# Expert choice in two batches, TensorE products that nothing reads, and a later read of the latent weights

## What is computed

```
h = h + pool_mixer(rmsnorm(h, a_norm)) ; h = h + hierarchical_moe(rmsnorm(h, ffn_norm[0]), ...)
k_nope, k_rope, v = shared_latent_kv(h, ...)
h = h + mla_mixer(rmsnorm(h, b_norm), ...) ; h = h + hierarchical_moe(rmsnorm(h, ffn_norm[1]), ...)
return rmsnorm(h, final_norm)[:, 16:]

# hierarchical_moe, the part that chooses
p_g = softmax(xf @ wr_g + br_g); g_sel = argmax(p_g); w_g = max(p_g)
sel = logit_e[g_sel]                      # 8 of the 32 experts' logits
top_v, top_i = top_k(sel, 2)
gate = w_g * softmax(top_v); eid = g_sel * 8 + top_i
# then rows are sorted by expert, every expert runs on its rows, and each token adds its two results
```

## Time and profile before

| what | value |
|---|---|
| median of 3 runs | 2169.54 us |
| the profiled execution's own time | 2170.03 us |
| its span, first to last instruction | 2168.3 us |
| PE busy | 1961.4 us (90%) |
| DVE busy | 809.5 us (37%) |
| ACT busy | 531.4 us (25%) |
| mean granted TensorE clock | 0.944 |

### The profile page before, as it was taken

One profiled execution on the slowest core, in us unless ns is written; L12 is line 12 of the kernel. 1 busy time (PEld: TensorE's weight loads), 2 busy tenths in 40 slices (PEclk: granted clock), 3 DMA queues, 4 the chain that ended last, 5 costly groups with the idle time before them and its releaser, 6 DMA issues. The chain is left out here.

```text
span 2168.3 us, 28117 instructions
## 1 busy us (share of the span) xinstructions
PE 1961.4 (90%) x10975; PEld 1146.7 (53%) x10975; DVE 809.5 (37%) x1863; ACT 531.4 (25%) x1290; POOL 189.3 (9%) x283
## 2 busy tenths in 40 slices
PE   8999999889997958999976999999999985999990
PEld 4545554478543944444434656777675553444440
DVE  1114556766353452111115534434352124111115
ACT  1003233433111311111122433333331110111112
POOL 0000002001162201000002000000000000000003
PEclk9999999889998967999998999999999986999995
DMA  3500100020021146999984000000010026999987
GB/s 136 213 34 11 39 20 4 1 81 4 2 98 44 49 204 245 404 423 425 424 368 158 23 1 1 1 1 1 1 78 23 29 81 278 379 426 423 425 354 263
DMA packets 51388, 334.66 MB, mean 154 GB/s; under 512 B 6832, under 2 KB 7152, under 8 KB 33200
## 3 DMA queue, kind: packets, MB, share of 16 engines
q1 hardware_dynamic: 39376, 289.63, 32.9%
q0 software_dynamic: 11872, 43.13, 5.5%
HBM read 285.48 MB, written 47.25 MB: 153 GB/s over the span
## 5 line engine op out<-in xcount | busy, mean ns | idle before, releaser
L221 PE MATMUL psum<-arena 128*128 128x512 f32 (+12 forms) x9584 | 1817.1, 384 | 117.5 <-DVE arena L2052 26.7
L221 PEld LDWEIGHTS psum<-arena 128*128 128x128 f32 (+3 forms) x9584 | 994.5, 169 | 887.3 <-issue 774.8
L2162 DVE TENSOR_TENSOR arena<-psum,arena 128x256 f32<-128x256 f32 x50 | 21.2, 425 | 429.5 <-ACT arena L2212 429.5
L1541 ACT ACTIVATE arena<-arena 128x1024 f32<-128x1024 f32 x43 | 45.4, 1056 | 255.1 <-DVE arena L2907 105.6
L2248 POOL DMA_INDIRECT arena<-xn_rows,arena x50 | 47.3, 945 | 672.4 <-PE psum L2123 447.9
L2212 ACT ACTIVATE arena<-psum 128x256 f32<-128x256 f32 x50 | 19.3, 385 | 327.6 <-PE psum L221 327.6
L2820 ACT ACTIVATE arena<-psum,arena 128x1024 f32<-128x1024 f32 (+8 forms) x72 | 50.2, 699 | 188.6 <-DVE arena L2856 188.6
L1242 ACT ACTIVATE arena<-psum 128x256 f32<-128x256 f32 (+3 forms) x128 | 44.0, 356 | 103.3 <-PE psum L221 92.2
L2205 ACT ACTIVATE arena<-psum 128x512 f32<-128x512 f32 x50 | 29.9, 597 | 148.0 <-PE psum L221 148.0
L2123 PE MATMUL psum<-arena 128*128 128x128 f32 x400 | 53.7, 279 | 10.0 <-DMA arena<-xn_rows,arena 10.0
L2849 DVE TENSOR_TENSOR psum<-psum,arena 128x128 f32<-128x128 f32 (+2 forms) x72 | 20.3, 283 | 103.5 <-PE psum L221 103.2
(11 more groups left out here) (304 smaller groups left out, 1303.4 us busy)
## 6 DMA issues: line engine op xcount, KB each, us to landing
arena<-in_w_exp SPq DMA_DIRECT2D x64, 2048.0 KB, 20.0
arena<-in_w_exp SPq DMA_DIRECT2D x64, 1024.0 KB, 19.9
expert_rows<-arena SPq DMA_DIRECT2D x66, 512.0 KB, 15.3
arena<-in_x SPq DMA_DIRECT2D x16, 512.0 KB, 4.1
xn_rows<-arena SPq DMA_DIRECT2D x16, 512.0 KB, 2.6
arena<-in_w_out SPq DMA_DIRECT2D x8, 512.0 KB, 7.7
arena<-in_w_o SPq DMA_DIRECT2D x1, 4096.0 KB, 13.1
out<-arena SPq DMA_DIRECT2D x8, 512.0 KB, 5.6
```

The lines of the kernel that those rows point to most:

```text
L221: return e.matmul(out, lhsT, rhs, start=start, stop=stop, skip_group_check=True)
L1541: return e.activation(junk, h[:, s, :], ACT.Square, accum_out=sq_sum[:, s:s + 1])
```

## The change

1. `dve_table`'s first half becomes `dve_select(e, y, a, b)`, which works on the tiles a to b. It is called twice: for 0 to `first` (6 in layer 0, 7 in layer 1) inside the routing loop, and for the rest after it. The gates become `dve_gates`, after the second call, with one reciprocal in place of two. ScalarE does four exponentials in place of two.
2. TensorE gets `keep_busy`: n products of the identity with itself, four times side by side (512 columns), into bank 7, which nothing reads. Five stand ahead of the rank products, once all banks of the routing loop are empty; eleven behind the counts; five behind the index products; in layer 0 thirteen more after the last expert block.
3. `sp_latent_behind` moves behind SP's wait for the expert count and waits for the gathered rows of the first two tiles. DVE scales these weights ahead of the combines of tiles 4 and 5 in place of 2 and 3.

```diff
+            y.first = 6 if layer == 0 else 7
...
+        def dve_select(e, y, a, b):
+            ns = b - a
+            at = slice(a, b)
...
+            e.memset(y.gp[:, at, :], NEG).then_inc(*V.up())
+            after()
+            e.wait_ge(*y.rb.empty(("lg", y.slots.index(b - 1))))
...
+            if a == 0:
+                e.memset(y.before[:, 0, :], 0.0).then_inc(*V.up())
+            for s in range(a, b):
+                after()
+                e.tensor_tensor(y.before[:, s + 1, :], y.before[:, s, :], y.both[:, s, :], ALU.add).then_inc(
+                    *(y.before_in if s == y.ns - 1 else V).up())
+
+        def dve_gates(e, y):
...
+            e.wait_ge(*y.exp.at(4))
+            e.tensor_reduce(y.wg, y.eg, AX.X, ALU.add).then_inc(*V.up())
+            e.tensor_scalar(y.rr, y.e1, 1.0, None, ALU.add).then_inc(*V.up())
...
+            dve_select(e, y, y.first, ns)
+            dve_gates(e, y)
...
         def act_table(e, y):
-            for t, n in ((y.eg, 1), (y.e1, 2)):
-                e.wait_ge(*y.to_exp.at(n))
-                e.activation(t, t, ACT.Exp).then_inc(*y.exp.up())
+            for n, at in enumerate((slice(0, y.first), slice(y.first, y.ns))):
+                for u, t in enumerate((y.eg[:, at, :], y.e1[:, at])):
+                    e.wait_ge(*y.to_exp.at(2 * n + u + 1))
+                    e.activation(t, t, ACT.Exp).then_inc(*y.exp.up())
+
+        def keep_busy(e, bank, n):
+
+            for _ in range(n):
+                mm(e, four(bank), ident, bc_mid(ident, 4), True, True)
 
         def pe_table(e, y):
             ns = y.ns
+            wait_all(e, y.rb.totals)
+            keep_busy(e, banks[7], 5)
             e.wait_ge(*y.ids_g.at(2))
             e.wait_ge(*y.before_in.at(1))
...
             mm(e, y.tb.bank["count"][:, 0:NE], ones, y.before[:, ns, :], True, True).then_inc(*y.tb.fill("count"))
+            keep_busy(e, banks[7], 11)
             for s in range(ns):
...
             m.then_inc(*y.tb.fill("idx"))
+            keep_busy(e, banks[7], 5)
...
         def sp_latent_behind(e):
...
+            for s in range(2):
+                for j in range(2):
+                    e.wait_ge(*m_cl[s][j])
             e.dma_start(w_uq, io["w_uq"]).then_inc(d_lu.sem, 16)
...
             sp_store(e, y, NM - 1)
-            if y.n == 0:
-                sp_latent_behind(e)
...
-                if (d, s) == (0, 2):
+                if (d, s) == (0, 4):
                     e.wait_ge(*m_lu)
...
-                if (d, s) == (0, 3):
+                if (d, s) == (0, 5):
                     e.wait_ge(*m_uk)
...
             pe_experts(e, y)
+            if y.n == 0:
+                wait_all(e, y.ex.totals)
+                keep_busy(e, banks[7], 13)
             pe_over(e, y)
...
                 dve_route(e, y, d, p)
+                if (d, p) == ((y.norm_at, y.ns - 1) if y.n == 0 else (y.norm_at + 2, y.ns - 2)):
+                    dve_select(e, y, 0, y.first)
             dve_table(e, y)
...
             sp_over(e, y)
+            if y.n == 0:
+                sp_latent_behind(e)
```

More of the change, by code:

```diff
@@ L1686, in plan_layer @@
             else:
-                y.to_exp, y.exp, y.hot = layers[0].to_exp.after(2), layers[0].exp.after(2), layers[0].hot.after(2 * NS)
+                y.to_exp, y.exp, y.hot = layers[0].to_exp.after(4), layers[0].exp.after(4), layers[0].hot.after(2 * NS)
                 y.before_in, y.m_cnt, y.sorted = layers[0].before_in.after(1), layers[0].m_cnt.after(1), layers[0].sorted.after(NE // 8)
@@ new lines, in dve_gates, with after @@
+        def dve_gates(e, y):
+            ns = y.ns
+            def after():
+                e.wait_ge(*V.last())
+            e.wait_ge(*y.exp.at(4))
+            e.tensor_reduce(y.wg, y.eg, AX.X, ALU.add).then_inc(*V.up())
+            e.tensor_scalar(y.rr, y.e1, 1.0, None, ALU.add).then_inc(*V.up())
+            after()
+            e.tensor_tensor(y.rr, y.rr, y.wg, ALU.mult).then_inc(*V.up())
+            after()
+            e.reciprocal(y.rr, y.rr).then_inc(*V.up())
+            after()
+            e.tensor_copy(gates[:, 0:ns, 0:1], y.rr.unsqueeze(2)).then_inc(*V.up())
+            e.tensor_tensor(gates[:, 0:ns, 1:2], y.rr.unsqueeze(2), y.e1.unsqueeze(2), ALU.mult).then_inc(*V.up())
@@ L1923, in after @@
                 e.wait_ge(*V.last())
-            def largest(x):
-                for s in range(ns):
-                    e.max(y.m8[:, s, :], x[:, s, :]).then_inc(*V.up())
-                for s in range(ns):
-                    if s == 0:
-                        after()
-                    e.max_index(y.i8[:, s, :].bitcast(U32), y.m8[:, s, :], x[:, s, :]).then_inc(*V.up())
-            e.memset(y.gp, NEG).then_inc(*V.up())
-            after()
-            e.wait_ge(*y.rb.empty(("lg", y.ns - 1)))
@@ L1954, in dve_table @@
-            largest(y.me)
-            after()
-            v0, v1 = (y.m8[:, :, j:j + 1].rearrange("p a b -> p (a b)") for j in range(2))
-            e.tensor_tensor(y.e1, v1, v0, ALU.subtract).then_inc(*y.to_exp.up())
-            e.wait_ge(*y.exp.at(2))
-            e.tensor_scalar(y.rr, y.e1, 1.0, None, ALU.add).then_inc(*V.up())
-            after()
-            e.reciprocal(y.rr, y.rr).then_inc(*V.up())
-            after()
-            e.tensor_tensor(y.rr, y.rr, y.wg, ALU.mult).then_inc(*V.up())
@@ L1964, in dve_table @@
-            after()
-            e.tensor_copy(gates[:, 0:ns, 0:1], y.rr.unsqueeze(2)).then_inc(*V.up())
-            e.tensor_tensor(gates[:, 0:ns, 1:2], y.rr.unsqueeze(2), y.e1.unsqueeze(2), ALU.mult).then_inc(*V.up())
-            e.tensor_copy(y.ei, y.i8[:, :, 0:2].bitcast(U32)).then_inc(*V.up())
-            for j in range(2):
-                after()
-                e.tensor_tensor(y.oh[j], bc_mid(y.io32, ns), y.ei[:, :, j:j + 1].to_broadcast([P, ns, NE]), ALU.is_equal).then_inc(*V.up())
-                after()
-                e.tensor_tensor(y.oh[j], y.oh[j], bc_last(y.valid, NE), ALU.mult).then_inc(*V.up())
@@ L1973, in dve_table @@
-            after()
-            e.tensor_tensor(y.both, y.oh[0], y.oh[1], ALU.add).then_inc(*V.up())
-            e.memset(y.before[:, 0, :], 0.0).then_inc(*V.up())
-            for s in range(ns):
-                after()
-                e.tensor_tensor(y.before[:, s + 1, :], y.before[:, s, :], y.both[:, s, :], ALU.add).then_inc(
-                    *(y.before_in if s == ns - 1 else V).up())
+            dve_select(e, y, y.first, ns)
+            dve_gates(e, y)
             def eight(r, left):
```

53 lines of the change are left out of this document (35 added, 18 removed).

## The result

The changed kernel took 2147.68 us (median of 4 runs, 2144.10 to 2152.09), the kernel before 2169.90 in the same comparison. The ratio is 0.9903, 95% interval 0.988 to 0.9926: faster, by about 1%. The profiled execution took 2145.41 us, its span is 2143.7 against 2168.3. So the two profiled executions differ by 24.6 us, the medians by 22.2; the forecast was 17.1. PE is now busy for 2004.4 us (94%), DVE for 812.5, and the mean granted clock is 0.964 instead of 0.944.

What follows compares the result with a forecast made beforehand. PE's waits for DVE's chain in both tables and at the latent start bound the kernel; in expert blocks PE and DMA nearly tie. 7.8 + 5.9 + 3.4 = 17.1 us gave 2152.4 us, range 2145.5 to 2160.

Steps and rivals of the forecast that it cites:

- three signs that the forecast itself named for being wrong: PEclk 0.5 through the eleven products; first gathers of 8 us or more; first block's lead still there at blocks' end.
- Choice in two batches, layer 0: Layer 0's table: six tiles chosen early, three after; running counts ready at 792.4 instead of 799.2 us.
- The five ahead of the ranks: Before the rank products: raise the clock, ranks take 1.2 instead of 2.45 us; layer 0's DVE goes on 6.8 us earlier.
- Eleven: Behind the counts: need 9.7 us within a 13.85 us gap, hidden; nothing would be longer without them.
- The last five: Behind layer 0's index products: delay PE 1.5 us, warm start saves 4.0; only 1.0 us of lead counted, bounds 0 and 2.5.
- rival (a): PE, not the reads, sets the end of the expert blocks, so the remaining lead passes: 2149.9 us; chance 0.15.
- Latent weights: Latent start: first gathers faster without weight reads beside them, tile 0's combine ends 5.9 us earlier; bounds 0 and 7.
- Thirteen: After layer 0's last expert block: clock expected to have fallen again before the latent transposes; value 0, at best 3 us.
- rival (b): The thirteen products do keep the clock up into the latent stage: 3 us more, 2149.4 us; chance 0.05.
- Layer 1: Layer 1's table and first blocks: rank copy 2.9 us earlier plus 0.5 from the last five, 3.4 us.
- Rival (d): Identity products do not raise the clock in the tables, so the kernel gets slower: 2183.5 us; chance 0.03.

Runs made afterwards that it cites:

- e4: Changed kernel without the five products ahead of the ranks, in both layers: 2145.26 us, ratio 0.9868 to the kernel before.
- e8: Changed kernel with six tiles chosen first in layer 1 and only the last five products kept: 2151.73 us, ratio 0.9906 to the kernel before.
- e1: Changed kernel with all added identity products removed in both layers: 2157.53 us, ratio 0.9928 to the kernel before.
- e2: Changed kernel without the five products behind the index products, in both layers: 2156.78 us, ratio 0.9924 to the kernel before.
- e3: Changed kernel with ten products instead of five behind the index products, in both layers: 2159.42 us, ratio 0.9939 to the kernel before.
- e6: Changed kernel with latent weights again read behind the last expert store and scaled ahead of tiles 2 and 3: 2155.81 us, ratio 0.9927 to the kernel before.
- e7: Changed kernel whose latent weight reads do not wait for the first two tiles' gathered rows: 2155.36 us, ratio 0.9926 to the kernel before.
- e10: e9 without the thirteen products: 2146.16 us, ratio 0.9884 to the kernel before.
- e9: Changed kernel without the five products ahead of the ranks and with six tiles chosen first in layer 1: 2146.58 us, ratio 0.9889 to the kernel before.
- e5: The changed kernel itself, unaltered, run again: 2149.17 us, ratio 0.9903 to the kernel before.
- e11: e9 with twelve products for eleven and a small identity product behind each index product but the last: 2153.60 us, ratio 0.9911 to the kernel before.
- e12: e9 with four products instead of five behind the index products: 2144.72 us, ratio 0.9879 to the kernel before.

## Why the prediction was right, and where it was off

**Direction, path and order of size** were right: 17.1 us forecast, 22.2 measured. But one of the three signs that the forecast itself named for being wrong came true: the first block's lead is still there at the end of the blocks. Term by term:

- *Choice in two batches, layer 0.* Rank copy 6.8 us earlier, forecast 6.8. The counts were ready at 9.8 + 5.6 = 15.4 us after the last normalized row's start (forecast 15.7), the five products began at 785.44 and the copy came 2.8 us behind the counts.
- *The five ahead of the ranks.* Counted as free in layer 0 and as 3 us of the price in layer 1. e4 shows what they are: a loss of 0.3 and 1.6 us. The forecast had the numbers for this (794.85 without them against 794.8 with) and did not draw the conclusion.
- *Eleven.* Hidden, as forecast, but not quite worthless: "if they were not there nothing would be longer" is off by 0.7 to 0.8 us of A (e8); e1 against e2, with the first five's 0.3 us allowed for, gives 0.5. In layer 1 it holds.
- *The last five, and the step that failed*: "The reads' own train starts with the gathered rows, 6.8 us early. It already hands over at the last moment, so of this lead I count 1.0 us". All of it passed: A fell by 10.5 us, B did not grow. Only the fourth expert's read waits for gathered rows; the next is issued when PE is done with a buffer. It went out at 842.22 before and at 830.58 after, 11.64 us earlier, just as the second block's transposes; the fourth expert's own, at 832.67 before and 823.64 after, came only 9.03 us earlier and held nothing back. Every read behind it is tied to PE in the same way, so a read that lands 0.1 us before its block does so after any shift. The price of the delay was 0.6 us against 1.5 forecast, and the gain of the warm start 4.0, as forecast; the term is 10.5 - 6.8 = 3.7 instead of 1.0. Of the 2.7 us between them 1.5 are the lead counted as given back, 0.9 the smaller delay and 0.3 the cast, which was 7.1 us early and not 6.8. This was rival (a), with 0.15; e2 and e3 decide for it. Its own wording, that the 0.6 us wait at 1087 would go, was wrong: it is still there.
- *Latent weights.* 7.3 instead of 5.9, just outside the bounds (0 to 7). The gathers gave what was forecast: 4.3 us for the first and 1.4 for the second, forecast 4.2 and 1.7. The missing 1.6 us come with the last store, which landed that much sooner, a step that the forecast did not have. Seven of the eleven profiles without reads beside the gathers have the early landing; in the other four C is 16.4 to 17.2, that is 5.0 to 5.9 us won. e6 and e7 show the cause as forecast.
- *Thirteen.* 0 was forecast, and e10 against e9 agrees (D 28.0 and 28.3, medians 0.4 us apart). The forecast's reason does not hold throughout: it expected 4.9 us between their end and the transposes and a clock fallen by then (before the change it had fallen 4.0 us after PE's last product, not under 4); the wait was 3.4 us, and in three profiles, both of the changed kernel among them, the clock had not fallen (1.09 us), in five it had (1.97). Since D is 28.2 to 28.3 in those three and 30.5 to 30.9 in those five, a worth of up to 2.3 us in some executions is not excluded, which is rival (b). The Trainium skill, "TensorE: Matmul & The Clock Gate", section "HAM oscillation", says that a burst behind a long wait starts cold each time; over waits of 3.2 to 3.5 us the traces agree with it in three profiles of six, and over the waits of 5.6 and 5.7 us (e2, e4) in both.
- *Layer 1.* 4.9 us to the second transposes, and 0.8 in the blocks, where a wait of 1.6 us for a read shrank to 0.7: 5.7 against 3.4. The 0.8 are chance (F is 286.3 to 289.7 over all runs). The rank copy was 3.3 us early (2.9 forecast); the rest is again the lead that passed.
- *Rival (d)* is out: the clock rose in each group of identity products. The Trainium skill, "TensorE: Matmul & The Clock Gate", section "PE-mode transpose", says that transpose mode does not count as busy for the clock; that concerns another mode, and no run here tests it.

Sum by measured terms: 10.5 + 7.3 + 5.7 = 23.5, and 1.1 from the stretch ahead of the change, which is chance: 24.6, the difference of the two profiles. The medians' 22.2 is the better measure of the change; the three terms without the chance 0.8 give 22.7, and some 21 where the last store lands late.

## What to carry to other kernels

A transfer that lands at the last moment is no bound by itself: ask who issues it. If the engine that needs it also frees its buffer, both move together and a lead ahead of the loop passes in full; that a fixed start would take it back is plausible, but no run here shows it. Work that nobody reads pays where it delays its queue by less than the work at full clock right behind it saves (the last five delay 0.6 and 1.3 us, save 4.0 and 2.6, and are worth 3.1 and 1.7 by e2); ahead of a short product it costs more than it gives. And a large row of waiting time says where to look, not what is to be won: the first five and the thirteen fill 7.6 and 12 us of waits (e4, e10), and no time won is shown for either.

## What the runs showed of the hardware beyond that

- The wait in front of the last shared block is 0.4 to 2.1 us in both layers of all profiles, whatever PE's lead is. Six of these waits were 2.06 to 2.12 us long; behind four of them (layer 0 of e4 and e5, layer 1 of e7 and e11) the granted clock fell within the block behind the wait (in e5 it is 0.51 from 1078 to 1081) and the block took 1.7 us more, behind the other two (e8, e12), and all shorter ones, it did not. So a late read can be paid twice. Why the read is late in some executions stays open.
- The first gather of 512 KB took 4.3 to 4.5 us with no reads beside it (changed kernel, twice) and 8.5 to 9.8 with 4.25 MB of reads issued 3.0 to 5.7 us ahead of it (before, e6, e7). The reads that were put behind it made the fourth tile's gathers slow instead (the second of them issued at 1135.05, landed at 1148.71), where PE has work and waits for none of it.
- B and F differ by up to 3.6 us and D by 3 where kernels are equal there. Ratios from four to six executions have intervals of some 5 us either way; differences of 1 us had to be read from intervals between two instructions, which repeat within 0.2 us.
